# Sample-state transfers behind the third weight half of the next group on the load queue of a hybrid decoder layer

## The reference, cut to what matters

```
z = einsum('btd,de->bte', rms_norm(x), w_in)          # all paths
# RWKV-7 heads, for each position:
sa = einsum('bhij,bhj->bhi', S, a_t)
S  = S * w_t + sa (x) b_t + v_t (x) k_t
y  = einsum('bhij,bhj->bhi', S, r_t)
# attention heads: three dilated windows, merged; the samples read caches of 2048 keys and values
y  = x + einsum('bte,ed->btd', concat(rwkv, attention), w_out)
```

## Time and profile before

| | |
|---|---|
| median of 3 runs | 1535.91 us |
| the profiled execution's own time | 1539.49 us |
| its span | 1537.7 us |
| TensorE matmul busy | 1453.0 us, 94% of the span |
| VectorE, ScalarE, GpSimd busy | 45%, 34%, 38% |
| mean granted TensorE clock | 0.974 of full speed |

### The profile page before, as it was taken

How to read it: one execution, slowest core, us unless ns; L and a number is a source line. 1 busy time by engine, 2 the same in 40 slices (tenths; PEclk the granted TensorE clock), 3 DMA queues, 4 the chain that set the end, 5 groups by cost and what they waited for, 6 DMA issues and landing times.

```text
span 1537.7 us, 34267 instructions
## 1 busy us (share of the span) xinstructions
PE 1453.0 (94%) x14670; PEld 1360.1 (88%) x14670; DVE 692.5 (45%) x1447; ACT 515.8 (34%) x857; POOL 579.1 (38%) x740
## 2 busy tenths in 40 slices
PE   5999899898998989989899999999999999699998
PEld 4999799898998989989799989899899988599998
DVE  6136374563745637456374353363443544410000
ACT  6142242322423224232242344444444443322221
POOL 6452241322413224132242344344344343764442
PEclk8999999999999999999999999999999999899999
DMA  6331220312203122031221655555366374444451
GB/s 201 81 102 31 69 67 14 94 41 69 67 14 92 43 70 67 14 99 37 70 78 35 140 125 142 121 136 125 87 146 148 96 171 99 145 125 121 129 153 55
DMA packets 252068, 143.08 MB, mean 93 GB/s; under 512 B 12093, under 2 KB 244990, under 8 KB 251390
## 3 DMA queue, kind: packets, MB, share of 16 engines
q1 hardware_dynamic: 228300, 125.90, 32.2%
q10 hardware_dynamic: 23618, 15.00, 3.3%
HBM read 125.36 MB, written 15.45 MB: 92 GB/s over the span
## 4 chain that ended last, share of the span: by engine, by line
PE 81%; DVE 5%; DMA 4%; issue 2%; ACT 1%; SPq 1%; POOL 1%; DVEq 0%; ACTq 0%
PE acc L482 55%; DMA WR<-in_w_in 3%; PE head_banks L922 3%; PE head_banks L927 2%; PE head_banks L912 2%; PE head_banks L864 2%; PE head_banks L1066 1%; PE head_banks L1086 1%; PE head_banks L1079 1%; PE head_banks L1113 1%; PE head_banks L1035 1%; PE head_banks L831 1%; PE head_banks L879 1%; PE head_banks L978 1%; PE head_banks L990 1%
## 5 line engine op out<-in xcount | busy, mean ns | idle before, releaser
L465 POOL TENSOR_TENSOR WL<-WR,WH 128x256 fp32r<-128x256 f32 (+1 forms) x656 | 507.2, 804 | 912.9 <-ACT WH L455 884.0
L482 PE MATMUL acc<-XH,WH 128*128 128x260 f32 (+1 forms) x2624 | 578.4, 302 | 11.1 <-POOL WL L465 6.4
L482 PE MATMUL acc<-XH,WL 128*128 128x260 f32 (+1 forms) x2624 | 531.4, 284 | 0.0
L482 PE MATMUL acc<-XL,WH 128*128 128x260 f32 (+1 forms) x2624 | 531.0, 284 | 0.0
L482 PEld LDWEIGHTS acc<-XH,WH 128*128 128x128 f32 (+1 forms) x2624 | 408.1, 190 | 47.3 <-issue 33.5
L482 PEld LDWEIGHTS acc<-XL,WH 128*128 128x128 f32 (+1 forms) x2624 | 408.0, 190 | 0.0
L482 PEld LDWEIGHTS acc<-XH,WL 128*128 128x128 f32 (+1 forms) x2624 | 406.8, 189 | 0.0
L455 ACT ACTIVATE WH<-WR 128x1024 fp32r<-128x1024 f32 (+1 forms) x164 | 171.5, 1048 | 167.7 <-PE acc L482 114.9
L490 ACT ACTIVATE AREN<-acc 128x520 f32<-128x520 f32 (+1 forms) x82 | 49.4, 602 | 367.6 <-PE acc L482 360.1
L1901 DVE TENSOR_TENSOR AREN<-head_banks,AREN 128x512 f32<-128x512 f32 x16 | 11.1, 692 | 167.0 <-PE head_banks L1137 167.0
L1442 ACT ACTIVATE AREN<-head_banks 128x128 f32<-128x128 f32 (+3 forms) x64 | 28.0, 438 | 103.0 <-PE head_banks L1079 102.6
(11 more groups left out here) (237 smaller groups left out, 1683.3 us busy)
## 6 DMA issues: line engine op xcount, KB each, us to landing
WR<-in_w_in SPq DMA_DIRECT2D x128, 512.0 KB, 5.3
WR<-in_w_out SPq DMA_DIRECT2D x32, 512.0 KB, 7.0
out<-AREN ACTq DMA_DIRECT2D x32, 256.0 KB, 3.3
AREN<-in_cache_k_win SPq DMA_DIRECT2D x16, 384.0 KB, 8.4
AREN<-in_cache_v_win SPq DMA_DIRECT2D x16, 384.0 KB, 9.1
mix_scratch<-AREN ACTq DMA_DIRECT2D x16, 260.0 KB, 4.2
AREN<-in_x_prompt SPq DMA_DIRECT2D x4, 1024.0 KB, 7.6
AREN<-in_cache_k_win SPq DMA_DIRECT2D x8, 512.0 KB, 7.1
```

What stands on the lines that cost most here:

```text
L465: rest = pool.tensor_tensor(WL[:, place, j:j + 2, 0:M], WR[:, k % 4, j:j + 2, 0:M], WH[:, place, j:j + 2, 0:M].bitcast(F32), ALU.subtract)
L482: mm = pe.matmul(acc[0:M, hf, 0:HT], w[:, (4 * g + k) % 3, j, 0:M], x[:, kt, hf * HT:(hf + 1) * HT], start=(kt == 0 and n == 0), stop=(kt ...
```

## The change

The two state transfers move on SyncE's queue. Before, `states(i)` and `states_out(i-1)` followed half 7 of one group, and so stood ahead of half 0 of the next. Now they follow half 2 of the next group. For the last RWKV pair, whose next group is the first attention group, they stand behind that group's first three halves. No instruction is added or removed, and no wait is changed.

```diff
             for i in range(1, PAIRS):
                 for k in range(8):
                     load_half(sp, group_a(i), k, w_half(OFF_A[k // 2], i, k))
+                    if k == 2 and i > 1:
+                        states(i - 1)
+                        states_out(i - 2)
                     if k == 3:
                         lora_up(i)
-                states(i)
-                states_out(i - 1)
...
             for k in range(3):
                 load_half(sp, group_b(0), k, w_half(OFF_B[k // 2], 0, k))
+            states(PAIRS - 1)
+            states_out(PAIRS - 2)
             group_b_on(0)
             states_out(PAIRS - 1)
```

## The result

Four runs of the changed kernel gave 1489.78 us as their median (1487.68 to 1490.0), four of the kernel before 1537.26 us: a ratio of 0.9688, 95% interval 0.9659 to 0.9717. By the medians of the three comparisons the change makes the kernel 47 to 53 us faster. The profiled execution took 1489.81 us.

The account below looks back on a forecast made before the run. TensorE was taken as the bound, busy 1453.0 of 1537.7 us, with stalls from late weight loads. Removing 37.1 us of waits and 14.9 of lower clock, 52.0 off 1535.91, gave 1484 us, range 1478 to 1492.

Parts of the forecast that it names:

- The cause: End of RWKV pairs: TensorE's L978 waits 37.1 us in all, as half 0's load stood behind the store awaiting "ry".
- The 6.07 us of landing: Half 0's load in pair 3: time from issue to landing, taken as that of four loads sharing the DMA engines.
- The size of the stall: L964 to L1003 of chunk 3, pairs 0 to 6: 106.04 us would shrink to pair 7's 7.72 each, 52.0 us less.
- The lower clock: TensorE behind L978's wait: granted clock 0.50 costs 2.1 us a pair and would go with the wait.
- the 14.9 us: Chunk 3, pairs 0 to 6: part of the 52.0 us beyond the 37.1 us wait, ascribed to the lower clock.
- Half 3, S0's load and the store at no cost: SyncE's queue: these transfers still land in time, half 3 with 17.7 us left, the store's reader 18.8 us after issue; 0.
- The rounding in front of the copy at 0: ScalarE between L1308 and L1311: the 1.05 us rounding shows no TensorE gap; taken as 0, bounds 0 and 7.4 us.
- The sum: Whole kernel: 37.1 + 14.9 = 52.0 us off 1535.91 gives 1483.9, forecast as 1484 us.
- A remnant of the stall: Rival at L978: the rounding shows as a gap, 1491 us, or the lower clock stays, 1499; chance 0.05.
- no effect: Rival on SyncE's queue: something else holds half 0 until "ry", so the time stays 1536 us; chance 0.02.
- half 3 late: Rival at the next pair's start: half 3 lands after ScalarE wants it; 1569 us at ten microseconds late; chance 0.01.
- Without its pauses TensorE is granted less: Rival in stage A: losing the 52 us again needs 104 us at the 1.2 GHz level; slower, chance 0.01.

Follow-up runs that it names:

- e1: Changed kernel, but S0's load stays ahead of half 0 and only the store moves behind half 2: 1490.01 us, 0.9684 of the kernel before.
- e2: Changed kernel, but the store stays ahead of half 0 and only S0's load moves behind half 2: 1538.84 us, 0.9997 of the kernel before.
- e6: Changed kernel, but SyncE holds half 0 until VectorE's "p4", 0.7 us earlier than "ry": 1508.90 us, 0.9826 of the kernel before.
- e5: Changed kernel, but SyncE holds half 0 until VectorE's "ss2", 2.5 to 3.2 us earlier than "ry": 1495.26 us, 0.9721 of the kernel before.
- e7: Changed kernel, but half 3 stands behind the lora matrices: 1485.32 us, 0.9669 of the kernel before.
- e4: Changed kernel unaltered, timed again in the first group of experiments: 1487.68 us, 0.9672 of the kernel before.
- e10: Changed kernel unaltered, timed again in the third group, five rounds: 1489.15 us, 0.9673 of the kernel before.
- e3: Changed kernel, but both state transfers stand behind half 0 and not half 2: 1489.26 us, 0.9684 of the kernel before.
- e9: Changed kernel, with half 3 of the second attention group also moved ahead of the last store, constants and six cache loads: 1484.60 us, 0.9642 of the kernel before.
- e8: Changed kernel, but half 3 stands behind the lora matrices and is held until TensorE's "tail": 1521.95 us, 0.9898 of the kernel before.

## Why the prediction was right, point by point

- **The cause.** Right in that the store in front of half 0 held it, and only the store: shown by e1 and e2. The prediction put the whole of the lateness on the wait for "ry"; by e6 some 2.6 of the 5.3 us were the store's own issue and transfer. The 6.07 us of landing were not those of a burst of four loads, as it took them: behind the store and without loads behind it half 3 of the changed kernel took 5.7 us, and in e5, with a burst behind it and no store ahead, half 0 took 4.0. As the change takes the whole store out of the way, neither moved the forecast.
- **The size of the stall.** Seven stretches of 7.72 us were forecast from pair 7 and came: 106.04 - 7 x 7.72 = 52.0 us left them.
- **The lower clock.** The forecast that the 14.9 us would go with the wait held: the granted clock is 1.00 in all eight stretches. Not all of the 14.9 us were the clock: a wait at the unchanged clock lengthens the stretch by some 0.27 us beside its counted length (e6, pair 2: 9.71 - 7.72 - 1.72), which would be about 2 us of them.
- **Half 3, S0's load and the store at no cost.** Right; e7 gives half 3's room as 17 us or more.
- **The rounding in front of the copy at 0.** Right: no gap.
- **The sum.** 1484 us was forecast and 1489.78 measured, inside the range of 1478 to 1492. Three sizes in it were off. The base was the median of three runs, 1535.91; the kernel before gave 1536.45 to 1540.36 in the three groups of the experiments. The 52.0 us taken off it were those of one execution, which itself lay 3.6 us above that median; in e2 the same seven waits cost 48.8. By ratio the forecast was 1483.9 / 1535.91 = 0.9661, which lies in the intervals of all three comparisons. And the span became 49.7 us shorter, not 52.0. From the store of pair 0 to that of pair 7 it went from 672.41 us (180.03 to 852.44) to 623.07, 49.3 less. Of the 2.7 us missing there, the store of pair 6 came 91.60 us after that of pair 5, where 88.53 separate those of pairs 0 and 1: 3.1 us. They lie at 691 to 698 us, where the granted clock was 0.50 with TensorE busy and no wait in front. What TensorE did before was the run of small matmuls (64 x 64 x 32) of the recurrence's set-up with gaps of 0.15 to 0.18 us. The term left out is that the clock may fall without a stall. It doesn't belong to a place in the program alone: e4 and e10, with the same code, didn't show it, and the same gaps stand in every pair. In the traces of e1, e3, e4, e9 and e10 and the changed kernel's own it fell in stage A once in 48 pairs. All three sizes made the forecast too low. Taken off the profiled execution's own time the prediction's sum was 1487.5 us, 2.3 us below the 1489.81 us of the profiled execution after.
- **The rivals.** A remnant of the stall, no effect, and half 3 late are out by the traces. "Without its pauses TensorE is granted less" is out too: the mean granted clock rose from 0.974 to 0.987. What remains of it is the one fall in pair 6.

How the clock decides to fall in one pair and not in another stays open; e4, run for this, showed only that the fall need not come.

## What to carry to other kernels

In a queue that is one list in order, ask of each instruction that waits what stands behind it and when that is wanted: here a store whose reader came 26 us later held a load that could have left 52 us earlier. A pair of the same loop that happens to be free of the wait is a good estimate of what the wait costs, since it has the clock in it: 7.72 us here, and 7.72 or 7.73 came. Its size is that of one execution, so take it off that execution's own time. And a wait of TensorE was worth more than its counted length in every case here: 52.0 us for 37.1 in the kernel before, 48.8 for 36.7 in e2, and 2.0 for 1.7 us at the unchanged clock in e6.

## What the runs showed of the hardware that was not expected

- What stands right ahead of a load on its queue lengthens its landing, be it a store or a load. A 512 KB weight load took 6.0 to 6.1 us to land right behind a 256 KB store (the kernel before, e2, e3) or a 256 KB load (e1), with a burst behind it, and 5.7 us behind the store with no load close behind it (half 3 of the changed kernel). With no state transfer ahead of it, it took 4.0 us (e5) and 4.6 us (e6: issued 454.58, rounded 459.15) with a burst behind it, and 4.0 to 5.1 us alone (halves 0 to 2 of the changed kernel). So the store cost its wait and, beside it, some 1.5 to 2 us of the load's own time.
- TensorE's granted clock fell to 0.50 behind all fourteen waits of 5.2 to 5.3 us (the kernel before and e2), five of seven of about 3.3 us (e8), and two of seven of 1.6 to 3.1 us (e6), but at the turn to stage B behind all ten of 1.6 to 4.3 us and not behind one of 1.2; once it fell behind gaps of no more than 0.18 us. So the length of a wait alone doesn't tell whether it falls.
